# Two transformer trunks in one kernel: the second network's attention regrouped into 12 steps, the modulation chunks moved

## What is computed

```python
proj = h @ w_in            # 1956 columns: q,k,v of FOX and MOBA (4 heads each), a forget logit, c_q 256, c_kv 128, k_r 32
o_f = dense_causal_attention(q_f, k_f, v_f, cumsum(log_sigmoid(f_logit + b)))   # 4 heads
o_m = moba_attention(q_m, k_m, v_m, t5_table)                                  # 4 heads; at 256 tokens causal plus a bias
q_lat = rmsnorm(c_q) @ w_uq ; kv = rmsnorm(c_kv) @ w_ukv                       # 8 heads of 96 (64 + 32 rotated)
o_c = dense_causal_attention(q_c, k_c, v_c)
o = concat([rmsnorm(o_f), rmsnorm(o_m), rmsnorm(o_c)]) @ w_out
x = x + gate * rmsnorm(o) ; then a SwiGLU MLP with hidden width 2816
```

## Time and profile before

| | us |
|---|---|
| runs: median of 3 (lowest, highest) | 2060.65 (2054.01, 2063.05) |
| profiled execution, whole | 2062.21 |
| its span, first to last instruction | 2060.4 |
| PE busy | 1817.9 (88%) |
| DVE busy | 1160.3 (56%) |
| ACT busy | 691.5 (34%) |
| POOL busy | 116.5 (6%) |
| DMA read from memory | 306.50 MB |

### The profile page before, as it was taken

The page is one execution under the profiler, slowest core; times in us unless marked ns, Lnnn a source line. Parts: engine busy times, 40 slices in busy tenths (PEclk is TensorE's granted clock), DMA queues, the critical chain, the costliest instruction groups (busy, mean ns, idle before and its releaser), DMA issues.

```text
span 2060.4 us, 25840 instructions
## 1 busy us (share of the span) xinstructions
PE 1817.9 (88%) x10564; PEld 1460.7 (71%) x10564; DVE 1160.3 (56%) x1915; ACT 691.5 (34%) x883; POOL 116.5 (6%) x97
## 2 busy tenths in 40 slices
PE   5998987989999998979789979885999798859997
PEld 2775654768888887746579967444999684649996
DVE  2475455564454455654667664558665645486654
ACT  2423333241312223433343433342443233424431
POOL 1010002010000001100100000003000000030000
PEclk7998767999999999978899989887999999579999
DMA  8324455122322322344345536761564458215642
GB/s 317 122 83 164 164 205 184 41 103 82 110 94 82 121 66 95 130 164 164 113 167 181 204 131 227 273 239 50 176 198 162 154 213 298 70 49 177 198 163 89
DMA packets 172086, 310.26 MB, mean 151 GB/s; under 512 B 3232, under 2 KB 60576, under 8 KB 171328
## 3 DMA queue, kind: packets, MB, share of 16 engines
q1 hardware_dynamic: 168304, 295.03, 41.3%
q10 hardware_dynamic: 3376, 12.01, 1.7%
q0 software_dynamic: 288, 1.57, 0.2%
HBM read 306.50 MB, written 2.10 MB: 150 GB/s over the span
## 4 chain that ended last, share of the span: by engine, by line
PE 70%; DVE 17%; issue 5%; ACT 5%; DMA 2%; POOL 1%; DVEq 0%; ACTq 0%; SPq 0%; POOLq 0%
PE bank L503 52%; PE twin L503 14%; DVE arena L1059 4%; PE bank L512 4%; DVE ring_r L1059 3%; ACT arena L1689 2%; ACT arena_r L1689 2%; DMA ring<-in_w_mod 1%; DVE arena L1624 1%; DVE arena_r L1059 1%; POOL rs L1982 1%; DVE params L1059 1%; DMA ring<-in_w_in 1%; DVE params L1489 1%; DVE arena L1139 1%
## 5 line engine op out<-in xcount | busy, mean ns | idle before, releaser
L503 PE MATMUL bank<-arena_r 128*128 128x512 f32 (+2 forms) x2016 | 665.5, 374 | 4.7 <-DVE params L1505 4.4
L1059 DVE TENSOR_TENSOR ring_r<-ring,arena_r 128x4096 fp32r<-128x4096 f32 (+5 forms) x90 | 380.2, 4225 | 242.2 <-ACT arena_r L1689 242.1
L503 PEld LDWEIGHTS bank<-arena_r 128*128 128x128 f32 x2016 | 385.1, 191 | 74.1 <-DVE params L1505 5.1
L1689 ACT ACTIVATE arena_r<-ring 128x4096 fp32r<-128x4096 f32 (+5 forms) x92 | 322.6, 3507 | 339.4 <-PE bank L503 294.0
L503 PE MATMUL bank<-arena_r,actT_r 128*128 128x512 f32 (+5 forms) x768 | 267.5, 388 | 27.8 <-DVE ring_r L1059 17.4
L1689 ACT ACTIVATE arena<-bank 128x256 f32<-128x256 f32 (+6 forms) x236 | 109.0, 462 | 521.9 <-PE bank L503 411.9
L503 PE MATMUL twin<-actT_r,arena_r 128*128 128x256 f32 x1408 | 255.2, 284 | 0.5 <-DVE actT_r L1059 0.4
L503 PEld LDWEIGHTS twin<-actT_r,arena_r 128*128 128x128 f32 x1408 | 220.6, 193 | 1.0 <-DVE actT_r L1059 0.9
L503 PE MATMUL bank<-ring_r,arena_r 128*128 128x512 f32 x560 | 219.2, 391 | 0.0
L503 PE MATMUL bank<-ring_r,actT_r 128*128 128x512 f32 (+5 forms) x576 | 216.0, 375 | 0.0
L503 PE MATMUL twin<-actT_r,ring_r 128*128 128x256 f32 x704 | 199.6, 284 | 0.0
(11 more groups left out here) (165 smaller groups left out, 1804.4 us busy)
## 6 DMA issues: line engine op xcount, KB each, us to landing
ring<-in_w_mod SPq DMA_DIRECT2D x24, 2048.0 KB, 8.2
ring<-in_w_ada SPq DMA_DIRECT2D x24, 2048.0 KB, 8.0
ring<-in_w_gate_up SPq DMA_DIRECT2D x44, 1024.0 KB, 7.4
ring<-in_w_down SPq DMA_DIRECT2D x20, 2048.0 KB, 7.9
ring<-in_w_up SPq DMA_DIRECT2D x16, 2048.0 KB, 7.8
ring<-in_w_out SPq DMA_DIRECT2D x8, 2048.0 KB, 8.1
ring<-in_w_down SPq DMA_DIRECT2D x8, 1792.0 KB, 7.5
ring<-in_w_in SPq DMA_DIRECT2D x6, 2048.0 KB, 8.9
```

What stands on the lines that cost most here:

```text
L503: ins = nc.tensor.matmul(out_, lhsT, rhs, start=start, stop=stop)
L1059: return v.tensor_tensor(o, x, y, op)
L1689: return nc.scalar.activation(o, x, func, **kw)
```

## The change

**Order of loads.** Batches become 4, 16, 16, 8 and 4. In layer 0 of the first network, two chunks are taken within in1, 14 in attention, one behind out1 and eight in the MLP (one behind each pair of `up1` or `down1`). In layer 1, ten are taken in attention and one behind out1. Each layer of the second network takes four: one ahead of its first norm, three in the preparation. Their loads stand between the weights' own loads. `up2`, chunk 0, is loaded ahead of `out2`, half 1.

**Parameters** of the second network come in two parts, a small one early (`par2a`) and the large one (`par2b`) behind in2's third chunk.

**Second network.** The columns of w_in are put in another order, so that the latents and the forget logit come in the first chunk (420 columns), and the other three have 512. The preparation is placed between the chunks. Attention becomes 12 steps of 512 score columns (4 heads of the first query block or 2 of the second). A column of ones beside the values gives the row sum. Scores run four steps ahead of values, two of turned weights. The squares, scales and turns of the first half of the mixed tile move into the attention loop. `out2`, half 0, is split there by ACT and DVE in two parts (no longer by POOL), and its first half of products is taken ahead of the last norm.

The diff, cut to what is spoken of:

```diff
-CH2 = [(0, 490), (490, 980), (980, 1468), (1468, 1956)]
+CQ, CKV, KR, FL, LAT = 0, 256, 384, 416, 420
+CH2 = [(0, 420), (420, 932), (932, 1444), (1444, 1956)]
-PAR2 = [("w_uq", 1536), ("w_ukv", 1024), ("g_q_lat", 256), ("g_kv_lat", 128), ("g_group", 1024), ("b_forget", 4)]
+PAR2 = [("w_uq", 1536), ("w_ukv", 1024), ("g_group", 1024), ("g_q_lat", 256), ("g_kv_lat", 128), ("b_forget", 4)]
+PAR2_LATE = 3584
...
-BATCHES = [NFIRST, 16, 8, 12, 8]
+BATCHES = [NFIRST, 16, 16, 8, 4]
...
+BESIDE1 = [14, 10]
...
+    for l in range(L):
+        if l == 0:
+            out += [("in1", l, 1), ("par1", l, 0), ("in1", l, 2)] + take(1) + [("in1", l, 3), ("in1", l, 4)] + take(1)
+        else:
+            ins = [("in1", l, c) for c in range(len(CH1))]
+            out += ins[:2] + [("par1", l, 0)] + ins[2:]
+        out += take(BESIDE1[l]) + [("out1", l, 0)] + take(1) + [("out1", l, 1)]
+        for q in range(4):
+            for kind in ("up1", "down1"):
+                out += [(kind, l, 2 * q + i) for i in range(2)] + take(1 if l == 0 else 0)
+    for l in range(L):
+        ins = [("in2", l, c) for c in range(len(CH2))]
+        out += [("par2a", l, 0), ins[0]] + take(1) + ins[1:3] + [("par2b", l, 0)] + take(1) + ins[3:] + take(2)
+        out += [("out2", l, 0), ("up2", l, 0), ("out2", l, 1)]
+        out += [("up2", l, c) for c in range(1, F2 // 256)]
+        out += [("down2", l, c) for c in range(2 * len(HC2))]
+    assert not mods
...
+for l in range(L):
+    i = SPLITS.index(("up2", l, 0))
+    SPLITS[i:i + 2] = SPLITS[i + 1], SPLITS[i]
 def share(key):
-    if key[0] == "out2" and key[2] == 0:
...
-UNITS2 = [(kind, h, q) for q in range(TS) for kind, n in (("fox", 4), ("moba", 4), ("mla", 8)) for h in range(n)]
-SUMS2 = 25
+STEPS2 = [(kind, part[0], part[1]) for kind in ("fox", "moba")
+          for part in (((0, 1, 2, 3), 0), ((0, 1), 1), ((2, 3), 1))]
+STEPS2 += [("mla", (0, 1, 2, 3), 0), ("mla", (4, 5, 6, 7), 0)] + [("mla", (h, h + 1), 1) for h in (0, 2, 4, 6)]
+AHEAD = 4
...
+                if kind == "par2a":
+                    sp.wait_ge(slot_read, SPLITS.index(("down1", 1, 0) if l == 0 else ("up2", 0, 0)) + 1)
+                    sp.dma_start(params[:, PAR2_LATE:p2n], a["par2"][l, :, PAR2_LATE:p2n]).then_inc(late_in, 16)
+                    continue
+                if kind == "par2b":
+                    sp.wait_ge(x_ready, updates("par2", l))
+                    sp.wait_ge(slot_read, SPLITS.index(("in2", l, 0)) + 1)
+                    sp.dma_start(params[:, 0:PAR2_LATE], a["par2"][l, :, 0:PAR2_LATE]).then_inc(par_in, 16)
...
-                        sp.wait_ge(slot_read, sum(x not in MODS for x in order[:i - NSLOT + 1]))
+                        sp.wait_ge(slot_read, SPLITS.index(before) + 1)
...
+                if at == 0 and b > 0:
+                    pe.wait_ge(sums_ready, b)
...
-                if i < fills1(l):
+                if i < BESIDE1[l]:
...
+                    if l == 0 and j + 1 in (jobs_until(l, 3), jobs_until(l, 5)):
+                        fill()
...
+                fill()
                 normed(tiles1(l), 2 * l + 1)
...
+                    if l == 0:
+                        fill()
                     for half in range(2):
...
+                    if l == 0:
+                        fill()
...
+                def scores(j):
+                    kind, hs, q = STEPS2[j]
+                    n = P * (q + 1)
...
+                    b, filled = take("s")
+                    for e, h in enumerate(hs):
...
+                        mm(b[:, n * e:n * e + n], lhs, rhs, inc=filled if h == hs[-1] else None)
+                def weights_turned(j):
+                    pe.wait_ge(p2_ready, nth(p2_ready))
+                    b, filled = take("a")
+                    for c in range(4):
+                        tr(b[:, c * P:(c + 1) * P], SP[:, j % 2, c * P:(c + 1) * P], filled if c == 3 else None)
+                def values(j):
+                    kind, hs, q = STEPS2[j]
+                    done("a", mark["PT2", l, j])
+                    b, filled = take("v")
+                    for e, h in enumerate(hs):
+                        v_ = vv[:, :, h, :] if kind == "mla" else vfm[:, :, h + 4 * (kind == "moba"), :]
+                        contract(b[:, 65 * e:65 * e + 65],
+                                 lambda c: PT2[j % 2][:, ((q + 1) * e + c) * P:((q + 1) * e + c + 1) * P],
+                                 lambda c: v_[:, c, :], filled if h == hs[-1] else None, q + 1)
...
+                for c in range(2):
                     for t in range(TS):
+                        project(c, t)
...
+                for t in range(TS):
+                    project(2, t)
+                fill()
+                pe.wait_ge(qa_ready, nth(qa_ready))
+                done("a", mark["in2", l, 1, 1])
+                for hp in range(2):
+                    for src, r in ((qa, "v"), (ka, "a")):
+                        turned_heads(lambda t, h: src[:, 4 * t + h, :], "fox", 66, hp, r)
...
+                scores(0)
+                scores(1)
                 fill()
+                done("v", mark["in2", l, 2, 0])
+                done("a", mark["in2", l, 2, 1])
+                for hp in range(2):
+                    for at, r in ((0, "v"), (256, "a")):
+                        turned_heads(lambda t, h: qkm[:, t, at + 64 * h:at + 64 * h + 64], "moba", 64, hp, r)
                 fill()
+                project(3, 0)
+                weights_turned(0)
+                weights_turned(1)
+                scores(2)
+                scores(3)
+                project(3, 1)
+                done("v", mark["in2", l, 3, 0])
+                done("a", mark["in2", l, 3, 1])
+                for j in range(AHEAD, len(STEPS2) + AHEAD):
+                    values(j - AHEAD)
+                    if j - 2 < len(STEPS2):
+                        weights_turned(j - 2)
+                    if j < len(STEPS2):
+                        scores(j)
+                    if j == AHEAD:
+                        pe.wait_ge(heads_ready, nth(heads_ready))
+                        done("a", mark["kv", l])
+                    if j in (AHEAD, AHEAD + 1):
+                        for hp in (2 * (j - AHEAD), 2 * (j - AHEAD) + 1):
+                            for src, r in ((ql, "v"), (kc, "a")):
+                                turned_heads(lambda t, h: src[:, t, 96 * h:96 * h + 96], "mla", 96, hp, r)
+                    if j == 11:
...
+                done("v", mark["mix2", l, 0, 1])
+                gate(L + l, 2, 0, 0)
+                w = weights(("out2", l, 0))
+                banks = [take("v") for t in range(TS)]
+                for t, (b, filled) in enumerate(banks):
+                    for i in range(4):
+                        three(b[:, :], mixed(t)(i), [x[:, i, :] for x in w], i == 0, False)
                 pe.wait_ge(mixt_ready, nth(mixt_ready))
...
+                split(after(("in2", l, 1)))
+                dve.wait_ge(flog_ready, nth(flog_ready))
+                step(tt(lf[:, :, :], lf[:, :, :], lft[:, :, :], ALU.subtract), lf_ready)
...
+                def largest(j):
+                    kind, hs, q = STEPS2[j]
+                    n, at = P * (q + 1), 4 * (j % 2)
+                    b = filled("s")
+                    if q == 0:
+                        mask = t5[:, :, P:S] if kind == "moba" else bc(const("causal")[:, P:S], 1, 4)
+                        x = SP[:, j % 2, :].rearrange("p (h n) -> p h n", h=4)
+                        step(tt(x, b[:, :].rearrange("p (h n) -> p h n", h=4), mask, ALU.add), s_emptied)
+                        step(v.tensor_reduce(mx[:, at:at + 4], x, X_AXIS, ALU.max))
+                    else:
+                        for e, h in enumerate(hs):
+                            mask = t5[:, h, :] if kind == "moba" else const("causal")
+                            step(v.tensor_tensor_reduce(out=SP[:, j % 2, S * e:S * e + S], in0=b[:, S * e:S * e + S],
...
+                    step(v.tensor_scalar(nm[:, at:at + len(hs)], mx[:, at:at + len(hs)], -SCALE2[kind], None, ALU.mult),
+                         nm_ready)
+                for j in range(AHEAD, len(STEPS2) + AHEAD):
+                    weighted_sums(j - AHEAD)
+                    if j < len(STEPS2):
+                        largest(j)
+                    if j in (AHEAD, AHEAD + 1):
+                        for hp in (2 * (j - AHEAD), 2 * (j - AHEAD) + 1):
+                            turned_heads(qcT, 96, hp)
+                    if j in (9, 10):
+                        split_part(("out2", l, 0), j - 9)
+                    if j == 9:
+                        dve.wait_ge(par_in, nth(par_in, 16))
+                        for at, t, c0, c1 in two:
+                            squares(sq2[:, 0:c1 - c0], mix2[:, t, c0:c1], at)
...
+                    if j == 10:
+                        group_scales(two)
+                    if j == 11:
+                        for pr in range(2):
+                            b = filled()
```

(76 more changed lines are left out.)

469 lines of the change are left out of this document (216 added, 253 removed).

## The result

The changed kernel takes **2099.57 us** (median; 2098.95 to 2101.35) against 2060.48 in the same comparison: a ratio of 1.0196, 95% interval 1.0172 to 1.0220. It is 39 us slower. The forecast was 2065 with a range of 2032 to 2100, so the time lies at the very end of the range, far outside the forecast's own case (2052 to 2078).

The account below looks back on a forecast made before the run. PE was taken to set the pace, in late attention with many small matmuls at half clock. Losses of 57 us (layer 0's MLP) and 22 (rest) less 76 won (second network) gave +3 on 2062.2: 2065, range 2032 to 2100.

Parts of the forecast that it names:

- the forecast's own case: Whole kernel: the summed terms hold and the time is 2052 to 2078 us; chance 0.42.
- Part 1: Second network, first projection to MLP: 167 us against 208, 38 us won per layer, 76 in all (50 to 98).
- The wait of 6 us ahead of the third chunk: in2, second network: chunk 2's late load delays DVE's and ACT's work, so PE waits 6 us.
- The loop: Second network's attention loop: estimated at 45 us, between 38 (bound by DVE) and 55 (PE at half clock).
- the 5 us of wait ahead of the fourth chunk: in2, second network: chunk 3 lands late, DVE empties the needed bank only behind its split, PE waits 5 us.
- Part 2: First network, layer 0's MLP: modulation chunks 12.6 us, bank waits from late loads 36.2 and 2, clock 6; 57 us lost.
- The out1 terms: out1's half 1, first network: late weights cost 8.4 us in layer 0 and 7.8 us in layer 1.
- I add 6 us for half clock behind these gaps: Layer 0's MLP, first network: matmuls slowed to half clock after PE's bank waits cost 6 us in all.
- Part 3: The rest, +22 us (8 to 27): out1 waits, extra fills, and +2.1 in layer 0's in1 and attention.
- C: Half clock through the whole attention loop (+20), more clock lost behind PE's waits (+8): 2093 us; chance 0.22.
- D: Attention loop at full clock, bound by DVE, 38 us (-14), out2's first half at full clock (-6): 2045; chance 0.22.
- B: Weights don't wait, DVE or loads have unseen slack; bank waits and after-effects vanish: 2007 us; chance 0.10.

Follow-up runs that it names:

- e1: Changed kernel, but in layer 0's MLP and out1's second half DVE empties the first two tiles' banks before splitting the next weights: 2037.33 us.
- e2: Changed kernel with the eleven modulation chunks of layer 0's in1, out1 and MLP (first network) moved into its attention: 2020.36 us.
- e10: e1's edit on top of e9, as a control: 1967.19 us.
- e8: e1 and e3 together, plus layer 1's modulation chunk between out1's halves (first network) moved into that layer's attention: 2007.76 us.
- e3: Changed kernel with up2's first chunk loaded and split behind out2's second half again, as in the kernel before: 2077.89 us.
- e6: e2 and e3 together on the changed kernel: 1999.79 us.
- e7: e6 plus e8's move, and the second network's four modulation chunks per layer loaded behind the projection chunks and multiplied in the attention loop: 1971.74 us.
- e9: e7 with two modulation chunks moved from layer 1's attention to layer 0's (first network; 27 and 9): 1962.11 us.

## Why the prediction was wrong

**Right.** Part 1: 38 us won in each layer, 39.4 and 36.8 measured. The wait of 6 us ahead of the third chunk was 5.96. The loop ran from 1797.1 to about 1844, 47 us for 45. Some luck is in this total: the 5 us of wait ahead of the fourth chunk never came (its load took 9.1 us where I had 12.3, so its split was done 4 us earlier), and the 7.3 us for the scaled groups, which I had nowhere, stood in the loop instead. Part 2's mechanism and its waits: 36.2 + 2 us forecast, 37.6 us more idle time measured. There are seven waits of 4.7 to 6.2 us and one of 0.8, where I had seven (three of 6.2 and four of 4.4) and one of 2; four turned out to be of the long kind. e1 and e2 remove these waits in two different ways, and e10 shows that the order alone isn't worth anything. The out1 terms, 8.4 and 7.8, came out at 7.7 and (e8) 7.4; but e1 shows that in layer 0 the bank wait isn't a price by itself, for without it the wait for the norm is longer by nearly as much.

**Wrong, by size.** The term "I add 6 us for half clock behind these gaps" measured 15.8 (same matmuls, 389.85 against 374.06 us busy). The rows had given 2.5 us for a gap and 17 in all, and I took a third of it, for no reason that a row gave. This is the place where the prediction weighed the Trainium skill's rule (page TensorE: Matmul & The Clock Gate, section HAM oscillation — how this bites in real kernels): bursts parted by waits for transfers fall back to 1.2 GHz in each of them. With that rule the trace agrees: the granted clock is 0.50 behind each of the seven long waits, and the price is 15.8 us. The fills there cost 17.0 us of PE and 13.9 of time, where 12.6 stood.

**Wrong, by omission.** The swap of `up2`'s first chunk with out2's second half stood in the diff, and I gave it no line at all. It cost 9.7 and 9.6 us (e3), 15.3 of which show between the two kernels, because e3's FFNs are also shorter than before's. It is the very mechanism of Part 2, a load that takes the slot of the chunk ahead of its predecessor and so is issued one chunk later, at a chunk that lasts only 11 us. I had worked this out for `down1`, out1 and in2 and didn't run the same rule over the rest of the order.

**Wrong, by size, a second time.** In Part 3, in1 and attention of layer 0 were to lose 2.1 us: 5.7 for the late fourth chunk, 1.9 for one fill, less 5.5 that "two fewer in attention give back". They lost 7.7. The late chunk cost 5.3. From there to the first attention step (171.55 us before, 181.33 after) the rest of in1 with its one fill took 4.5 us more and not 1.9; from that step to out1 the attention took 191.3 us instead of 193.3, so the two fewer gave back 2.1. PE waits in this attention anyway, and with 25 or 27 chunks there a chunk costs 0.5 to 1.0 us (198.4 to 203.1 us for this part in e2, e6, e7, e9 and e10).

Together, measured less forecast: 13.2 in the MLP (9.8 of clock, 4.4 of fills, the idle time 0.6 under its term and the rest rounding), 5.6 in layer 0's in1 and attention, 15.3 by the swap, and -0.2 in all other terms: 33.9. By the spans it is 36.8 - 3 = 33.8.

**The rivals.** C gave 2093, nearly the measured time, mostly for a reason that didn't occur: the loop kept clock 1.00 until 1815 and 0.97 until 1825, and had 0.50 only in its last 20 us. Only C's small second term, more clock lost behind PE's waits, was right in kind. So it is a nearly right number with the wrong mechanism for most of it; its fix, work to keep the loop warm, would not have touched the MLP, where the 70 us were. D, too, is half true: full clock for most of the loop, but 47 us and not 38, 7.3 of them the wait for the scaled groups, and the last 20 at half clock. B is excluded by the waits themselves.

## What to carry to other kernels

In a ring of few slots, go through the whole written order once and note for each load what releases its slot and how long the chunk lasts that is to hide it; every place where something was put in or swapped moves the issue of the loads behind it. An engine that waits for a load holds up all that stands behind it in its program: put the emptying of PSUM banks ahead of the wait where loads can be late, or better, put filler loads where PE has idle time (here the attention, about 1 us or less for a chunk) and not where it is full (1.7 us for a chunk, and 56 more in all by the waits and the clock). And price a gap of PE with the clock behind it: here seven gaps of 4.7 to 6.2 us cost some 2.3 us each on top in slow matmuls (15.8 in all).

## What the runs showed of the hardware that I had not expected

- The clock's loss lies mostly behind the gap and not in it. In the 4.71 us gap up to 616.07 the granted clock was 1.00 until 616, and in the 5 us after it 0.66. In the 6 us gaps (up to 508.42, and in the FFN up to 1534) it had already fallen while PE stood, to 0.70 and 0.68 in the last stretches shown. In all of them it was 0.50 when the matmuls began again. A reader who looks at the stretch of the gap alone doesn't see what the matmuls behind it lose.
- It needs no long gap: seven waits of 4.7 to 6.2 us cost 15.8 us of clock, some 2.3 each. Before, the same stage had no such gap and ran at 1.00.
- The loads had room: 27 modulation chunks of 2 MB in the 267 us of layer 0 (e9) made no weights late (the chain into out1 there is DVE's and holds no load), while 11 in the 216.5 us of layer 1 (e7) made the next weights late and 9 didn't. I read this as the place of the last one in the queue deciding, more than the sum of the bytes; e9 changed both, so it isn't shown apart.
